# Two transformer blocks on one core: the conditioning of x in five groups, X loaded first, both halves of a partial sum moved by one instruction

## What is computed

```python
def first_block(x, c, w_ada, b_ada, norm1_w, w_in, ...):
    mod = jax.nn.silu(c) @ w_ada[l] + b_ada[l]
    shift1, scale1, gate1, shift2, scale2, gate2 = jnp.split(mod, N_MOD, axis=-1)
    h = rms_norm(x, norm1_w[l]) * (1.0 + scale1[:, None]) + shift1[:, None]
    proj = h @ w_in[l]                      # 2048 x 8192
    u_pool, q, k, v, g_a, g_b = jnp.split(proj, split_at, axis=-1)
    ...
```

## Time and profile before

| What | us |
|---|---|
| Median of 3 runs (lowest, highest) | 2602.59 (2600.03, 2607.41) |
| The profiled execution's own time | 2602.57 |
| Its span in the profile | 2600.8 |
| PE busy, share of the span | 2521.6, 97% |
| DVE busy | 2015.3, 77% |
| ACT busy | 1277.8, 49% |
| Loads, mean | 255 GB/s |

### The profile page before, as it was taken

How to read it: one execution, slowest core, us unless ns; L and a number is a source line. 1 busy time by engine, 2 the same in 40 slices (tenths; PEclk the granted TensorE clock), 3 DMA queues, 4 the chain that set the end, 5 groups by cost and what they waited for, 6 DMA issues and landing times.

```text
span 2600.8 us, 32612 instructions
## 1 busy us (share of the span) xinstructions
PE 2521.6 (97%) x12429; PEld 2112.8 (81%) x12429; DVE 2015.3 (77%) x2305; ACT 1277.8 (49%) x1657; POOL 272.3 (10%) x321
## 2 busy tenths in 40 slices
PE   6999999999999999999999999999999999999998
PEld 5877787878888888888877878887888888888887
DVE  6778879998978888898887798885766666665566
ACT  4544454434555445544445554465455544554453
POOL 1000120202030202002020001350000000020000
PEclk9999999999999999999999999999999999999999
DMA  9998869897989889897966765464567677766654
GB/s 350 334 344 316 286 196 352 322 330 251 324 279 322 316 305 333 274 354 261 330 206 223 233 199 182 146 217 154 186 210 229 224 227 231 230 211 193 189 189 149
DMA packets 298364, 663.66 MB, mean 255 GB/s; under 512 B 20752, under 2 KB 21104, under 8 KB 297184
## 3 DMA queue, kind: packets, MB, share of 16 engines
q1 hardware_dynamic: 294976, 650.21, 74.2%
q0 software_dynamic: 2656, 9.66, 1.1%
...
## 4 chain that ended last, share of the span: by engine, by line
PE 81%; DVE 9%; DMA 3%; issue 3%; ACT 3%; POOL 0%; SPq 0%; DVEq 0%; ACTq 0%
PE PS L638 80%; DVE WL L1509 3%; DVE ACC L1517 2%; ACT WH L1095 2%; DVE UQ L1509 1%; DMA RAW<-in_w_o 1%; DMA RAWX<-in_w_in 1%; PE PS L641 1%; DMA RAW<-in_w_in 0%; DMA RAWX<-in_w_o 0%; DMA RAW<-in_w_ada 0%; DVE acc L1509 0%; DVE hn L1517 0%; DVE AL L1509 0%; DMA RAW<-in_w_ff 0%
## 5 line engine op out<-in xcount | busy, mean ns | idle before, releaser
L1095 ACT ACTIVATE WH<-RAW 128x1024 fp32r<-128x1024 f32 x567 | 600.3, 1059 | 782.4 <-PE PS L638 609.9
L1509 DVE TENSOR_TENSOR WL<-RAW,WH 128x1024 fp32r<-128x1024 f32 x567 | 703.9, 1242 | 356.3 <-ACT WH L1095 355.7
L638 PE MATMUL PS<-WH,AH 128*128 128x512 f32 x2052 | 812.0, 396 | 17.8 <-DVE WL L1509 12.1
L638 PE MATMUL PS<-WH,AL 128*128 128x512 f32 x2052 | 800.4, 390 | 0.0
L638 PE MATMUL PS<-WL,AH 128*128 128x512 f32 x2052 | 799.9, 390 | 0.0
L638 PE MATMUL PS<-HL,WH 128*128 128x512 f32 x2048 | 723.8, 398 | 6.3 <-DVE HL L1517 5.1
L638 PE MATMUL PS<-HL,WL 128*128 128x256 f32 x2048 | 574.9, 281 | 0.0
L638 PEld LDWEIGHTS PS<-WH,AH 128*128 128x128 f32 x2052 | 386.1, 188 | 105.8 <-DVE WL L1509 22.1
L638 PEld LDWEIGHTS PS<-HL,WH 128*128 128x128 f32 x2048 | 384.6, 188 | 102.7 <-issue 9.0
L638 PEld LDWEIGHTS PS<-WH,AL 128*128 128x128 f32 x2052 | 385.6, 188 | 81.9
L638 PEld LDWEIGHTS PS<-WL,AH 128*128 128x128 f32 x2052 | 386.3, 188 | 76.8 <-issue 0.2
...
## 6 DMA issues: line engine op xcount, KB each, us to landing
RAW<-in_w_ff SPq DMA_DIRECT2D x335, 512.0 KB, 4.0
RAW<-in_w_ada SPq DMA_DIRECT2D x284, 512.0 KB, 5.1
RAW<-in_w_in SPq DMA_DIRECT2D x192, 512.0 KB, 4.5
RAWX<-in_w_ada SPq DMA_DIRECT2D x100, 512.0 KB, 5.3
RAWY<-in_w_ff SPq DMA_DIRECT2D x96, 512.0 KB, 4.1
RAWX<-in_w_ff SPq DMA_DIRECT2D x81, 512.0 KB, 5.2
RAWX<-in_w_in SPq DMA_DIRECT2D x48, 512.0 KB, 5.4
RAW<-in_w_out SPq DMA_DIRECT2D x32, 512.0 KB, 3.6
```

What stands on the lines that cost most here:

```text
L638: return e.matmul(o, l, r, start=start, stop=stop, skip_group_check=True)
L1095: return e.activation(o, i, f, **kw)
L1509: return e.tensor_tensor(o, a, b, op)
```

## The change

1. The conditioning comes in five groups: `GROUPS` = k-tiles 0-1, 2-3, 4-7, 8-11, 12-15. The 32 items of the first two are 128 x 512 numbers (256 KB, two runs of 1 KB for each partition), the others as before. `SUMS` is (0, 9, 22, 41, 61), and `PIECES` is cut anew: 12 pieces of a single tick first, 51 pieces in place of 40. The 16 items of group 1 stand among the first 8 chunks (two after each), group 2 among the next 13, group 3 among the next 19, group 4 among 20.
2. X is loaded ahead of the first "s" item. ACT loads the table of the square root before it waits for X. `keep_on` moves ahead of the turning of X and has 20 matmuls for 10.
3. Tick 0 orders its products by what each needs: both halves of AH x WH, then AH x WL, then AL x WH. DVE makes the low part of chunk 0 between the two parts of group 0.
4. A piece that is not a block's last ("part") is taken out by one instruction for both halves, one step after its last tick.

```diff
-PIECES = ([(n, 0, 2) for n in range(12)]
-          + [(n, 0, 4) for n in range(12, 16)] + [(0, 2, 4), (1, 2, 4)]
-          + [(0, 4, 6), (1, 4, 6)] + [(n, 2, 6) for n in range(2, 6)]
-          + [(n, 6, 8) for n in range(6)] + [(n, 2, 8) for n in range(6, 12)] + [(n, 4, 8) for n in range(12, 16)])
-SUMS = (0, 21, 41, 61)
+GROUPS = ((0, 2), (2, 4), (4, 8), (8, 12), (12, 16))
+PIECES = ([(n, 0, 1) for n in range(12)]
+          + [(0, 1, 2), (12, 0, 2), (1, 1, 2), (13, 0, 2), (2, 1, 2), (14, 0, 2), (3, 1, 2), (15, 0, 2), (4, 1, 2), (5, 1, 2)]
+          + [(0, 2, 4), (6, 1, 4), (5, 2, 4)] + [(n, 1, 4) for n in range(7, 10)] + [(10, 1, 3)]
+          + [(0, 4, 6), (1, 2, 6), (2, 2, 6), (5, 4, 6), (3, 2, 6), (4, 2, 6)]
+          + [(n, 6, 8) for n in range(6)] + [(n, 4, 8) for n in range(6, 10)]
+          + [(10, 3, 8), (11, 1, 8)] + [(n, 2, 8) for n in range(12, 16)])
+SUMS = (0, 9, 22, 41, 61)
...
-    plan += quarter[0]
+    plan += group[0]
...
-    for q in range(1, 4):
-        a, n = 20 * (q - 1), 20
+    for q, (a, n) in enumerate(((0, 8), (8, 13), (21, 19), (40, 20))):
         for i in range(n):
             plan.append(head[a + i])
-            plan += quarter[q][16 * i // n:16 * (i + 1) // n]
+            plan += group[q + 1][16 * i // n:16 * (i + 1) // n]
...
     def both(self, q):
...
-        return (name, n) in (("wo", 3), ("ff2", 31), ("ob", 3), ("fg2", 31)) or (name == "in2" and n >= 12)
+        return name == "part" or (name, n) in (("wo", 3), ("ff2", 31), ("ob", 3), ("fg2", 31)) or (name == "in2" and n >= 12)
...
-                if i == 1:
+                if i == 0:
                     e.dma_start(X[:, :, :], I["x"][0].rearrange("(t p) d -> p t d", p=128)).then_inc(s_x, 16)
...
+            keep_on(3, 20)
             for i in range(8):
                 b = 4 + i % 3
...
-                if j == 0:
-                    keep_on(3, 10)
...
+                    if j == 0:
+
+                        e.wait_ge(s_hi, 1)
+                        for x, y, what, count in ((AH, h, s_ah, k + 1), (AH, l, s_lo, 1), (AL, h, s_al, k + 1)):
+                            e.wait_ge(what, count)
+                            for t in range(2):
+                                m = mm(PS[:, b + t, :], x[:, k, t * 128:t * 128 + 128], y, kk == 0 and what is s_ah, False)
+                        continue
...
+            e.wait_ge(s_sq, 16)
+            preload_sqrt()
             e.wait_ge(s_x, 16)
...
+                    if name == "part" and bl.ev[q][t][0] == "act":
+                        if t == 0:
+
+                            e.wait_ge(s_wdone, done_at)
+                            af(in1_both(n), PS[:, bl.bank[q]:bl.bank[q] + 2, :], ACT.Copy).then_inc(s_ev["act"], 2)
...
+                            both = in1_both(n)
+                            tt(both, PS[:, bl.bank[q]:bl.bank[q] + 2, :], both, ALU.add).then_inc(s_ev["dve"], 2)
...
                     e.wait_ge(s_vc, 3)
-                    quarter(0)
+                    shift_and_scale(0, 0)
                     feed(0)
-                    quarter_low(0, 0, 1)
+                    shift_and_scale(0, 1)
+                    modulated_low(0, 0, 2)
```

More of the change, by code:

```diff
@@ L182, in weight_plan @@
     v = I["w_ada"][0].rearrange("(p t) (g n) -> p t g n", t=16, g=6)
-    quarter = [[("s", (q, t), v[:, t, 0:2, q * 512:(q + 1) * 512]) for t in range(16)] for q in range(4)]
+    group = [[("s", (q, t), v[:, t, 0:2, k0 * 128:k1 * 128]) for t in range(16)] for q, (k0, k1) in enumerate(GROUPS)]
     head = [c for n, c0, c1 in PIECES for c in w(I["w_in"][0], 2 * c0, 2 * (c1 - c0), n * 512)]
@@ L641, in turn, with keep_on @@
                 return e.transpose(o, i, ident)
+            def keep_on(bank, n):
+                for _ in range(n):
+                    mm(PS[:, bank, 0:128], ident, ident, True, True)
             def bank_free(q, t):
@@ L843, in root_rows @@
                 mm(PS[:, 0, 0:256], ones, rs[:, 0, :], True, True).then_inc(s_nR, 1)
-            def keep_on(bank, n):
-                for _ in range(n):
-                    mm(PS[:, bank, 0:128], ident, ident, True, True)
             def norm_gap(at):
@@ L1140, in _, with modulate @@
                 af(xT[:, 2 * i:2 * i + 2, :].rearrange("p a s -> p (a s)"), PS[:, 4 + i % 3, :], ACT.Copy).then_inc(s_xT, 1)
-            def quarter(q, k0, k1):
+            def modulate(q, k0, k1):
                 e.wait_ge(s_mod, 3 * summed(q, 0 if q or k1 == 1 else 1))
-                for k in range(4 * q + k0, 4 * q + k1):
+                for k in range(GROUPS[q][0] + k0, GROUPS[q][0] + k1):
                     a, b = MOD[:, 0, k:k + 1], MOD[:, 1, k:k + 1]
@@ L1484, in _ @@
                     for k0, k1 in sum_parts(0):
-                        quarter(0, k0, k1)
+                        modulate(0, k0, k1)
                 feed(j + look(j))
@@ L1493, in _ @@
                     evac(q, t)
-                for q in range(1, 4):
-                    if 0 <= j - SUMS[q] - 1 < 2:
-                        k0 = 2 * (j - SUMS[q] - 1)
-                        quarter(q, k0, k0 + 2)
+                for q in range(1, 5):
+                    k0 = 2 * (j - SUMS[q] - 1)
+                    if 0 <= k0 < GROUPS[q][1] - GROUPS[q][0]:
+                        modulate(q, k0, k0 + 2)
                 if j in norms:
@@ L1534, in item @@
                     q, t = info
[L1535 removed]
+                    acc = ACC[:, sum_at(q, 0, 0):sum_at(q, 2, 0)]
+                    raw = raw_at(i)[:, 0:sum_at(q, 2, 0) - sum_at(q, 0, 0)]
                     if t == 0:
@@ L1626, in evac @@
                 if name in ("in1", "part"):
-                    if bl.ev[q][t][0] == "dve":
+                    if name == "part" and bl.ev[q][t][0] == "dve":
+                        if t == 0:
+                            e.wait_ge(s_wdone, done_at)
+                            eng, count = evac_of[bl.sum_of[q]][1]
+                            e.wait_ge(s_ev[eng], count)
+                            both = in1_both(n)
+                            tt(both, PS[:, bl.bank[q]:bl.bank[q] + 2, :], both, ALU.add).then_inc(s_ev["dve"], 2)
+                    elif bl.ev[q][t][0] == "dve":
                         part = dst = in1_home(n, t)
@@ L2033, in _ @@
             tt(CS[:, 0:32], CS[:, 0:32], CS[:, 32:64], ALU.mult).then_inc(s_cs, 1)
-            for i in range(5):
+            for i in range(6):
                 item(i)
@@ L2037, in _ @@
             ts(SS[:, 10:12], SS[:, 8:10], 1.0 / D, EPS, ALU.mult, ALU.add).then_inc(s_n1, 1)
-            for i in range(5, 7):
-                item(i)
+            item(6)
             e.wait_ge(s_n1, 4)
@@ L2059, in _ @@
                     if j in SUMS[1:]:
-                        quarter(SUMS.index(j))
+                        shift_and_scale(SUMS.index(j), 0)
                     feed(j + look(j))
-                    for q in range(1, 4):
-                        if 0 <= j - SUMS[q] - 2 < 2:
-                            quarter_low(q, j - SUMS[q] - 2, 2)
+                    for q in range(1, 5):
+                        k0 = 2 * (j - SUMS[q] - 2)
+                        if 0 <= k0 < GROUPS[q][1] - GROUPS[q][0]:
+                            modulated_low(q, k0, k0 + 2)
                     for q, t in bl.ended(j - 2):
```

58 lines of the change are left out of this document (34 added, 24 removed).

## The result

| What | Before | After |
|---|---|---|
| Median of 20 runs each, taken together (lowest, highest), us | 2604.44 (2600.03, 2609.57) | 2609.47 (2603.75, 2613.22) |
| Ratio after to before, with its 95% interval | | 1.0015 (1.0008 to 1.0021) |

The account below looks back on a forecast made before the run. PE and the loads were taken to run side by side, both at their limit. The start's gain less later losses, 6.9 - 2.2 - 2.6 - 1.2 - 0.7, gave 0.2 us faster: 2602.4 us, range 2595 to 2609.

Parts of the forecast that it names:

- The start: Everything ahead of tick 0: X first and half-size items bring tick 0 to 30.9 us, 6.9 earlier.
- A load of 512 KB that finds the queue empty needs 3.7 us: Chunk loads in the early ticks: each lands 3.7 us after its issue, against 1.38 us in a full stream.
- the loop: Ticks 3 to 11: `WL` done, load, conversion, `WL` again take 6.1 us for two ticks, 3.05 a tick against 2.72.
- my own sign of being wrong: Trace after: tick 12 outside 68 to 75 us, or a shift over 3 us persisting or growing from tick 21.
- So it lands at 34.7: Chunk 2's load, asked for at 31.0 us, lands at 34.7; chunk 4's follows at 40.8.
- the wait ahead of tick 3: PE waits near 3 us there, as the first taking-out stands behind chunk 4's conversion; tick 3 at 43.0.
- the sum of group 1: Four PE matmuls before tick 12, said to lie in a stretch that waits anyway, so charged nothing.
- Chunk 21 lands at 91.3 at the earliest: Loads up to tick 21: 41 more units take 57 us from 34.7, leaving at most 3.1 us of gain.
- single-tick pieces starve PE, and its clock drops: Rival, ticks 1 to 12: 5.4 us loads and clock drops cost 10 to 11 us, giving 2613; chance 0.10.
- The rule on batching loads: 16 more loads, about 2.0 us fixed each, six in flight: 5.3 us more, 2607.5; weighed but not adopted.
- The ten more pieces: Extra DVE work over some 50 ticks, 12 us in all, mostly in DVE's free time; charged 0.7 us.
- X first does nothing: Rival, at the start: `keep_on` at 9.0 us puts tick 0 at 32.6, losing 1.5 us: 2604; inside the forecast's range.

Follow-up runs that it names:

- pair_keep12: pair_load with 12 instead of 20 `keep_on` matmuls ahead of the turning; 2604.26 us against 2604.05 for the kernel before, ratio 0.9996.
- chunks_first: The changed kernel with chunks 0 and 1 loaded ahead of group 1's items; 2609.49 us, ratio 1.0020 to the kernel before.
- pair_load: The changed kernel with two half-size items sharing one raw slot, same loads; 2605.88 us against 2604.62 for the kernel before, ratio 1.0003.
- less_bytes: pair_keep12 with items of groups 2 to 4 loading 256 KB for 512, so output differs; 2600.95 us against 2606.0 before, ratio 0.9988.
- second profile: The changed kernel, unaltered, profiled once more to show scatter; 2609.85 us.
- by_halves: The changed kernel without part 4, each half taken out by its own instruction; 2626.56 us against 2604.05 for the kernel before, ratio 1.0079.
- x_first_only: The kernel before with part 2 of the change alone; 2606.05 us against 2604.62, ratio 0.9999.
- before again: The kernel before, unaltered, profiled once more to show scatter; 2601.29 us.
- both_alone: The kernel before with part 4 of the change alone; 2604.16 us against 2605.06, ratio 0.9999.

## Why the prediction was wrong

The range ended 0.5 us below the result, and the forecast of 0.2 us faster was 5 us off.

**The start: right.** Tick 0 at 30.9; it was 31.01. `keep_on` 7.3 us from 13.6 to 20.9; it was 7.3, to 20.6. The turning 7.1; 7.3. An item chained 0.85; 0.86 (three of 0.75 in 2.46). X was later than forecast (10.82 for 9.7) and the scaled identity at 18.8 for 17.0, without effect, since `keep_on` held PE until then. That it was longer than X needs was in my text (20.9 against 17.0), but I did not follow what it cost; in pair_keep12 tick 0 began 1.6 us earlier and lost that again to the clock.

**The step that failed: "A load of 512 KB that finds the queue empty needs 3.7 us".** I took 3.7 us for each chunk of the loop, from a stretch at 340 to 375 us. The load of chunk 2 did take 3.5 (30.90 to 34.43), but chunk 3's took 5.2 and chunk 4's 5.3, and most others to 56 us near 5. Their queue is not empty: two items stand beside each chunk. The forecast has tick 3 at 43.0, tick 11 at 67.4 and tick 12 at 71.3, 0.9 earlier than before. Measured are 45.31, 71.9 and 75.86, which is 3.7 later than before. So the miss of 4.6 us is complete at tick 12, and my own sign of being wrong ("if tick 12 begins before 68 or after 75") came true there.

**"So it lands at 34.7" was right (34.4), but its sequel forgot chunk 3.** I followed the even chunks. Chunk 3 has the slot of chunk 1, whose `WL` stands behind two half-size items on DVE. It came at 40.4, and the wait ahead of tick 3, put at 3 us, was 4.3. That is 2.3 us of the miss.

**Two smaller terms were put at nothing, and they make up about the other 2.3 us.** The drop of the clock behind tick 3: I set it against the one before tick 0 in the kernel before, but that one is already in the 47.7 with which I compared. The new one had to be charged: 1.6, measured 1.7. And the sum of group 1, said to lie "in a stretch that waits anyway", lengthens tick 9 by 1.0. Without these two the loop would have been near my 3.05 us a tick (3.25 between the conversions of chunks 4 and 12, (69.23 - 43.20) / 8, with 1.7 us of slow clock in it). Neither decides alone: chunks_first has no slow clock at tick 3 and the same time.

**"Chunk 21 lands at 91.3 at the earliest": I took a full wire below it for granted.** It assumed 381 GB/s from 34.7 on. In 34 to 58 us there came 6 us x (250 + 293 + 319 + 299) GB/s = 7.0 MB, where 24 us x 381 GB/s would be 9.1: 2.2 MB short, 5.7 us. 91.3 + 5.7 = 97.0, and chunk 21's conversion, which waited for it, began at 97.27. PE had no wait from it; the same count at the chunk that PE did wait on says more. By chunk 13 there are 24 units behind the 16, so with a full wire it would land at 34.7 + 23 x 1.38 = 66.4; 5.7 us more are 72.1, and it landed at 73.0 (estimates, but for the last). I had counted the slots ("Of the six raw slots four now hold half-size items") and used it for the chunks that are there, but not for the bytes in flight. pair_load shows that it is in the main the fill of the slots: it alone brings the rate to 344 to 387 GB/s and takes 3.6 us off. less_bytes shows that behind this the full wire takes some 2.5 us of the lead, not all of it.

**The rival "single-tick pieces starve PE, and its clock drops"** (0.10, at 2613) named the nearest mechanism and its 5 us loads, though it put the loss on PE's loop. chunks_first speaks against that half: with the wait at tick 3 cut to 1.6 us the time is the same. The clock dropped once in these ticks, over 46 to 52 us (0.72, which is 1.7 us), not at every tick; in the second profile it dropped there and also at tick 0 (0.72 over 28 to 34 us). The Trainium skill, "TensorE: Matmul & The Clock Gate", section on HAM oscillation, tells of a kernel whose every batch of matmuls starts cold, and there the waits for loads are longer than the batches. The one drop in ticks 1 to 12 agrees with that: it follows the one wait that is longer than a tick (4.3 us). Behind it the waits are 1.3 us at most against ticks of 2.72, and the clock stays at 1.00. I had applied the section to a case that it does not describe. The drop at tick 0, with 1.35 us of waiting ahead of it, is not explained here.

**The rule on batching loads.** By the price that I worked out from the Trainium skill, "DMA: Bandwidth & Descriptors", the 16 loads more would make 2607.5 (rightly added, 2602.4 + 5.3 = 2607.7), which is nearer to the result than my sum. That is luck: pair_load has the same 16 loads more and is 3.6 us faster. The section on the anatomy of one DMA, which has these 2.0 us, is about DMAs that GpSimd issues, and here SP issues them. What counts here is how many bytes the slots keep under way, not a fixed part for each load.

**The ten more pieces**, charged with 0.7 us: from chunk 22 to 64 the changed kernel loses no more (+4.6, +4.0) and in its second profile 1.5 us more, so a cost of 0.7 is neither shown nor excluded; behind chunk 64 it is open (below). And this only with part 4; by_halves is 17 us slower. I had taken part 4 for a saved overhead, and it is what makes pieces of one tick possible.

**"X first does nothing"**: true by itself (x_first_only). Within the change it was not tried alone.

**The range.** Its terms, added, reach from 2596.7 (2602.4 - 3.1 - 2.6) to 2612.5 (2602.4 + 5.3 + 4.8); the 2609 does not follow from them. With its own sum the range would have held the result, and that would have been luck, as the upper 5.3 came from the rule on batching. A slip without effect: PE's three idle stretches ahead of tick 0 add to 23.4 us (12.9 + 8.4 + 2.1), not 22.

**What stays open.** Chunks 64 to 224: there the nine profiles with the new pieces lose another 1.9 to 4.8 us (the changed kernel 2.1: 217.0 to 221.0 became 730.6 to 736.6), while the three with the old ones (before again, x_first_only, both_alone) move by -1.0 to +0.8. By chunk 127, the last of the new order, it is -0.5 to +2.1; the greater part, 2.2 to 3.7, lies behind it, where no edit is (the old ones: 0.0 to +1.4). DVE is busy about nine tenths of that stretch. Whether the additional pieces on DVE do it, or only another phase between items and ticks, was not tried. Nor was the part of DVE's fixed order in the late release of slots. No version tried beats the kernel before while doing all of its work.
